# Output projection in two passes over the tokens, and a normalisation divided between it and the feed forward

## The reference

```python
y  = concat([out_a, out_b, out_c], -1) @ w_out[l]         # output projection; out_c is divided by its group RMS first
x  = layer_norm(ALPHA * x + g1 * y, ln1_g[l], ln1_b[l])   # g1, sh2, sc2, g2: adaLN vectors from c (c_ctx for the context)
h  = x * (1 + sc2) + sh2
x  = layer_norm(ALPHA * x + g2 * swiglu(h, w_gu[l], w_down[l]), ln2_g[l], ln2_b[l])
# the context tokens (ctx) go through the same in layer 0, and are dropped in layer 1
```

## Time and profile before

| | |
|---|---|
| median of 3 runs | 3813.87 us (3808.86 to 3818.49) |
| the profiled execution | 3815.01 us, span 3813.2 us, granted clock 0.944 |
| busy share | PE 88%, DVE 49%, POOL 36%, ACT 22% |
| stage out, layer 0, then layer 1 | from 927 to 1069 us, from 2889 to 3003 us |
| ffn up to the start of its second iteration | from 1070 to 1206 us, from 3004 to 3115 us |

### The profile page before, as it was taken

How to read it: one execution, slowest core, us unless ns; L and a number is a source line. 1 busy time by engine, 2 the same in 40 slices (tenths; PEclk the granted TensorE clock), 3 DMA queues, 4 the chain that set the end, 5 groups by cost and what they waited for, 6 DMA issues and landing times. The chain is left out here.

```text
span 3813.2 us, 47769 instructions
## 1 busy us (share of the span) xinstructions
PE 3362.3 (88%) x17208; PEld 2793.3 (73%) x17208; DVE 1866.7 (49%) x2854; ACT 846.7 (22%) x1574; POOL 1386.0 (36%) x1032
## 2 busy tenths in 40 slices
PE   0969989877979999999997669989787799999997
PEld 0849878655858888888884549878666578888885
DVE  8976534678582222222227886525675532222225
ACT  1136432212041010000003226432211220010102
POOL 1354222253324333343432254213242344444443
PEclk9979999988989999999998789999888899999998
DMA  7500002002301111111011410011002011111111
GB/s 278 171 17 1 0 30 65 6 20 89 118 28 39 39 39 39 33 41 42 33 33 67 171 61 1 0 39 56 6 14 86 33 40 49 50 50 50 44 50 50
DMA packets 63857, 197.74 MB, mean 52 GB/s; under 512 B 6160, under 2 KB 16656, under 8 KB 62736
## 3 DMA queue, kind: packets, MB, share of 16 engines
q1 hardware_dynamic: 54736, 172.32, 13.3%
q10 hardware_dynamic: 9024, 24.14, 1.8%
HBM read 177.05 MB, written 19.40 MB: 52 GB/s over the span
## 5 line engine op out<-in xcount | busy, mean ns | idle before, releaser
L188 PE MATMUL ps<-h_hi,f_whi 128*128 128x512 f32 (+1 forms) x1760 | 650.8, 370 | 26.5 <-DVE h_lo L1917 19.7
L189 PE MATMUL ps<-h_lo,f_whi 128*128 128x512 f32 (+1 forms) x1760 | 650.0, 369 | 0.0
L190 PE MATMUL ps<-h_hi,f_wlo 128*128 128x512 f32 (+1 forms) x1760 | 649.4, 369 | 0.0
L2145 DVE TENSOR_TENSOR f_gated<-f_gated,ps 128x512 f32<-128x512 f32 (+1 forms) x110 | 69.6, 634 | 973.8 <-PE ps L190 968.5
L2029 POOL TENSOR_TENSOR f_whi<-f_wraw,small 128x1024 fp32r<-128x1024 f32 x128 | 251.8, 1967 | 608.1 <-PE ps L190 608.1
L2153 DVE SCALAR_TENSOR_TENSOR x_res<-ps,mod,x_res 128x512 f32<-128x512 f32 (+1 forms) x440 | 306.8, 697 | 242.2 <-PE ps L190 241.9
L188 PEld LDWEIGHTS ps<-h_hi,f_whi 128*128 128x128 f32 x1760 | 333.3, 189 | 85.8 <-issue 22.2
L190 PEld LDWEIGHTS ps<-h_hi,f_wlo 128*128 128x128 f32 x1760 | 333.0, 189 | 55.8
L189 PEld LDWEIGHTS ps<-h_lo,f_whi 128*128 128x128 f32 x1760 | 333.3, 189 | 55.2
L188 PE MATMUL ps<-f_ahi,f_whi 128*128 128x512 f32 (+1 forms) x880 | 328.3, 373 | 0.0
L189 PE MATMUL ps<-f_alo,f_whi 128*128 128x512 f32 (+1 forms) x880 | 323.5, 368 | 0.0
(11 more groups left out here) (219 smaller groups left out, 6212.8 us busy)
## 6 DMA issues: line engine op xcount, KB each, us to landing
f_wraw<-in_w_ffn SPq DMA_DIRECT2D x132, 512.0 KB, 3.2
ada_w<-in_w_ada SPq DMA_DIRECT2D x80, 512.0 KB, 3.5
wrawc<-in_w_in SPq DMA_DIRECT2D x26, 512.0 KB, 3.8
wrawab<-in_w_in SPq DMA_DIRECT2D x16, 512.0 KB, 4.4
wrawo<-in_w_out SPq DMA_DIRECT2D x16, 512.0 KB, 3.4
ada_w<-in_w_ada ACTq DMA_DIRECT2D x16, 512.0 KB, 4.4
x_res<-in_xT SPq DMA_DIRECT2D x8, 640.0 KB, 6.5
x_spill<-x_res ACTq DMA_DIRECT2D x8, 640.0 KB, 5.6
```

The costliest lines, as they stand in the source:

```text
L188: pe.matmul(out, w_hi, h_hi, start=first, stop=False)
L189: pe.matmul(out, w_hi, h_lo, start=False, stop=False)
L190: return pe.matmul(out, w_lo, h_hi, start=False, stop=last)
L2145: dve.tensor_tensor(g, g, pl.bank(3 + c, tn), ALU.mult).then_inc(u_taken[c], 1)
```

## The change

`project_out` goes over the tokens twice. First it gathers and multiplies the early tokens (chunks 2 and 0; in layer 1 only chunk 0), output tiles 0 to 7; between those blocks PE turns the late tokens, chunk 1. Then it multiplies chunk 1, tiles 7 down to 0, in four banks that take turns. The last two weight tiles of the first pass serve the second as well; the other six are loaded and split again, so 14 tiles in place of 8. While the second pass runs, the early tokens are normalised: their mean and variance matmuls stand between its blocks, and centre, modulate and rest (in layer 1 the rescale too) stand among DVE's evictions. The first two weight tiles of the feed forward are loaded there too. The normalisation is now a class, `Norm`, with a step for each tile.

`feed_forward` normalises chunk 1 only, while PE runs gate and up of the early tokens for both inner tiles. Chunk 1 follows (for the second inner tile first, with a wait for each feature tile), which needs one weight tile once more. The rescale of the early tokens in layer 0 stands there as well. The 16 modulation tiles of layer 1 move out of layer 0's stage out into its ffn: `LaterModulation` does four products in each of iterations 1 to 8, with one buffer, its loads in ACT's queue and its products in DVE's.

```diff
--- before.py
+++ after.py
@@ -1628,137 +1628,411 @@
...
+        for k in range(KT):
+            dve.tensor_tensor(self.tile(c, k), self.tile(c, k), self.pl.bank(c, CHUNKS[c][1]),
+                              ALU.subtract).then_inc(self.centred[c], 1)
...
+    def modulate(self, dve, c, k):
...
+        dve.scalar_tensor_tensor(out=self.tile(c, k, self.pl.lo_f32), in0=self.tile(c, k),
+                                 scalar=self.gm[:, k, self.who(c)], in1=self.inverse(c),
+                                 op0=ALU.mult, op1=ALU.mult).then_inc(self.h_in[c], 1)
+
+    def rest(self, dve, c, k):
...
+        dve.scalar_tensor_tensor(out=self.tile(c, k, self.pl.lo), in0=self.tile(c, k, self.pl.lo_f32),
+                                 scalar=self.bm[:, k, self.who(c)], in1=raw(self.tile(c, k, self.pl.hi)),
+                                 op0=ALU.add, op1=ALU.subtract).then_inc(self.split[c], 1)
...
+    def block_bank(m, c):
+        return pl.bank(3 * (m % 2) + c if m < KT else (1, 4, 6, 7)[m % 4], CHUNKS[c][1])
+
+    def tile_of(m):
+
+        return m if m < KT else 2 * KT - 1 - m
+
+    def slot_of(m):
+        return m % 2 if m < KT else (m + 1) % 2
+
+    loads = [tile_of(m) for m in range(2 * KT) if m not in (KT, KT + 1)]
...
+                    sp.wait_ge(w_ready, m - 1)
+                sp.dma_start(w_raw[m % 2][:, :], a["w_out"][l, loads[m]]).then_inc(w_loaded[m % 2], 16)
+            load(0)
+            load(1)
+            sp.dma_start(pl.x[:, :, 0:width], pl.x_dram[:, :, 0:width]).then_inc(x_in, 16)
+            for m in range(2, KT + 2):
+                load(m)
+
+            sp.wait_ge(rest[1], len(items[1]))
+            for s in range(2):
+                sp.dma_start(ffn.early[s][:, :], a["w_ffn"][l, 0, s]).then_inc(next_in[s], 16)
+            for m in range(KT + 2, len(loads)):
+                load(m)
...
+            def split(p):
+                slot = p % 2 if p < KT else (p + 1) % 2
+                hi, lo = flat(w_hi[slot]), flat(w_lo[slot])
+                pool.wait_ge(w_loaded[p % 2], 16 * (p // 2 + 1))
+                if 2 <= p < KT:
+                    pool.wait_ge(full[0], p - 1)
+                elif p >= KT:
+                    pool.wait_ge(full[1], p - KT + 1)
+                pool.tensor_tensor(hi, w_raw[p % 2][:, :], one, ALU.mult).then_inc(w_rounded, 1)
+                pool.wait_ge(w_rounded, p + 1)
+                pool.tensor_tensor(lo, w_raw[p % 2][:, :], raw(hi), ALU.subtract).then_inc(w_ready, 1)
+            for p in range(KT + 1):
+                split(p)
+            for c in early:
+                norm.square_pairs(pool, c)
+            for p in range(KT + 1, len(loads)):
...
+            def multiply(m):
+                pe.wait_ge(w_ready, m + 1 if m < KT else max(KT, m - 1))
+                slot = slot_of(m)
+                for c in early if m < KT else late:
+                    t0, tn = CHUNKS[c]
+                    if 2 <= m < KT:
+                        pe.wait_ge(taken[c], m - 1)
+                    elif m >= KT + 4:
+                        pe.wait_ge(taken[c], m - KT - 3)
+                    for k in range(KT):
+                        mm = three_pass(pe, block_bank(m, c), w_hi[slot][:, k, :], w_lo[slot][:, k, :],
...
+            pe.wait_ge(rest[0], len(items[0]))
+            for m in range(KT):
+                multiply(m)
+                turn(1, m)
+            pe.wait_ge(rest[1], len(items[1]))
+            multiply(KT)
+            for c in early:
+                pe.wait_ge(norm.x_paired[c], KT // 2)
+                norm.mean(pe, c)
+            multiply(KT + 1)
+            norm.variance(pe, early[0])
+            multiply(KT + 2)
+            if not last:
+                norm.variance(pe, 0)
+            for m in range(KT + 3, 2 * KT):
...
+            for m in range(KT):
+                if m < 4:
+                    divide(1, m, m + 1)
+                evict(m)
+                rest_of(1, m)
+                if m % 2:
+                    for c in early:
+                        dve.wait_ge(taken[c], m + 1)
+                        norm.pair(dve, c, m // 2)
+            dve.wait_ge(next_rounded, 1)
...
+            evict(KT)
+            for c in early:
+                norm.centre(dve, c)
+            norm.invert(dve, early[0])
+            whole(norm.modulate, early[0])
+            whole(norm.rest, early[0])
+            evict(KT + 1)
+            evict(KT + 2)
+            if last:
+                norm.rescale(dve, 0)
+                evict(KT + 3)
+            else:
+                norm.invert(dve, 0)
+                whole(norm.modulate, 0)
+                evict(KT + 3)
+                whole(norm.rest, 0)
+            pair_late(3)
+            evict(KT + 4)
+            pair_late(2)
+            evict(KT + 5)
+            pair_late(1)
+            evict(KT + 6)
+            evict(KT + 7)
+            pair_late(0)
 
 
...
+    slot = [1, 0, 2, 1, 0, 2]
+    opening = [(0, early, 0), (1, early, 1), (2, early, 2), (3, early, 0),
+               (2, late, 2), (3, late, 0), (0, late, 2), (1, late, 1)]
+    blocks = [0, 1, 2, 3, 0, 4, 5]
+    homes = [0, 1, 2, 0, 2, 0, 2]
     n_down = KT * len(chunks)
     act_hi = pl.at(f"{tag}_ahi", [P, 2, TOK], F32R, kb=120)
     act_lo = pl.at(f"{tag}_alo", [P, 2, TOK], F32R, kb=130)
...
+            def split_opening(s):
+                pool.wait_ge(loaded[s % 2], 16 * (s // 2))
+                if s == 3:
+                    pool.wait_ge(gu_full[0], 1)
+                elif s >= 4:
+                    pool.wait_ge(gu_full[1], s - 2)
+                split(s - 1, s % 2, homes[s])
```

The opening of the feed forward on POOL, PE and DVE:

```diff
+            split_opening(2)
+            norm.square_pairs(pool, 1)
+            split_opening(3)
+            act_rest(0, 0, early)
+            act_rest(0, 1, early)
+            split_opening(4)
+            split_opening(5)
+            split_opening(6)
+            act_rest(0, 1, late, turn=0)
...
+
+            norm.mean(pe, 1)
+            for s, (j, part, place) in enumerate(opening):
+                if s == 1:
+                    norm.variance(pe, 1)
+                    pe.wait_ge(second_ready, 1)
+                elif s in (2, 3):
+                    pe.wait_ge(ready, s + 1)
+                elif s == 6:
+                    pe.wait_ge(ready, 5)
+                gate_up(0, j, part, place, None if s < 4 else (s - 4) // 2, norm.split[1] if s == 4 else None)
+            pe.wait_ge(ready, 7)
+            down(0, (homes[5], homes[6]))
...
+            norm.centre(dve, 1)
+            norm.invert(dve, 1)
+            for k in range(KT + 2):
+                if k < KT:
+                    norm.modulate(dve, 1, k)
+                if k == (2 if last else 4):
+                    gate(0, 0, early)
+                if k >= 2:
+                    norm.rest(dve, 1, k - 2)
+            gate(0, 1, early)
+            if carried is not None:
+                for c in early:
+                    carried.rescale(dve, c)
+                gate(0, 1, late, turn=0)
+                norm.rescale(dve, 1)
+            else:
+                norm.rescale(dve, 1)
+                gate(0, 1, late, turn=0)
+            gate(0, 0, late, turn=1)
+            if carried is not None:
+                for c in early:
+                    dve.wait_ge(carried.x_done[c], KT)
+            dve.wait_ge(norm.x_done[1], KT)
+            for c in chunks:
+                add(0, c)
+            for first, end, cond in loops:
+                with dve.Fori(first, end) as i:
+                    if cond is not None:
+                        ada.product(dve, cond, i, 0)
+                        ada.product(dve, cond, i, 1)
+                    gate(i, 0, chunks)
+                    if cond is not None:
+                        ada.product(dve, cond, i, 2)
+                        ada.product(dve, cond, i, 3)
```

And the products of layer 1's modulation, in DVE's queue ahead of the first gate product and between the first and the second (ACT's `ada.load` stands likewise, each load waiting for the product before it):

```diff
+                    if cond is not None:
+                        ada.product(dve, cond, i, 0)
+                        ada.product(dve, cond, i, 1)
+                    gate(i, 0, chunks)
+                    if cond is not None:
+                        ada.product(dve, cond, i, 2)
+                        ada.product(dve, cond, i, 3)
+                    gate(i, 1, chunks)
```

More of the change, by code:

```diff
@@ new lines, in _ @@
+            for p in range(2):
+                for n, (k, c) in enumerate(items[p]):
+                    t0, tn = CHUNKS[c]
+                    act.wait_ge(turned[p], n + 1)
+                    act.activation(pl.hi[:, k, t0:t0 + tn], pl.bank(gather_bank(p, n), tn), ACT.Copy,
+                                   scale=1.0 if k < 4 else gnorm(k)).then_inc(rounded[p], 1)
+            act.wait_ge(next_in[0], 16)
+            act.activation(ffn.hi[0][:, :], ffn.early[0][:, :], ACT.Copy).then_inc(next_rounded, 1)
@@ new lines, in _, with whole @@
+            dve.wait_ge(next_rounded, 1)
+            dve.tensor_tensor(ffn.lo[0][:, :], ffn.early[0][:, :], raw(ffn.hi[0][:, :]), ALU.subtract) \
+                .then_inc(next_split, 1)
```

(7 more changed lines are left out.)

550 lines of the change are left out of this document (361 added, 189 removed).

## The result

The changed kernel takes 3771.95 us (median of 4 runs, 3763.31 to 3779.39) for 3814.26 before: ratio 0.9886, 95% interval 0.9868 to 0.9905. I had said 3773. A second set of four gave 3771.65, ratio 0.9892 (0.9875 to 0.9908). The profiled run of the first set is its slowest, 3779.39; of the second, 3772.15.

A forecast was written before the change was run, and what follows sets the result against it. PE, 88% busy, was taken as the bound, waiting mainly in the gather and ffn's opening normalisation. Layer 0's 21.1 us and layer 1's 20.0 won, together 41.1 from 3815.0, gave 3773.9, so 3773 against the median; range 3747 to 3797.

The forecast's parts named there:

- Gather of layer 0: Ahead of layer 0's products: 12 divisions first, then rests, so products start 6.6 us earlier; layer 1's 11.0 earlier.
- 2.1 with none in the way: Layer 1's gather: division time in us if no POOL instruction intervenes; about 6 expected, 9.8 with all four.
- First passes: Early tokens' output products, with the wait for chunk 1's last rests: 75.4 us in layer 0, 51.2 in layer 1.
- Second pass of layer 1: Late blocks beside early normalisation: 43.6 of blocks, 6.8 of mean and variance, 11.3 of waiting, clock and last pair: 61.7 us.
- POOL's step is shut out until modulate and rest are over: Layer 1's second pass: tile 3's split waits behind DVE's 10.7 us stream, so PE waits 9.1 us, plus 1.7 of clock.
- My first rival: POOL gets its turn between DVE's instructions, so 22.3 us of waits and clock losses go: 3751 us; chance 25%.
- Second pass of layer 0: Late blocks 43.6, means and variances 10.2, waits of 0.6 and 2.8 us: 57.2 us.
- Gaps: Barrier from last product to first mean, with a last eviction, a pair and the stage change: 3.1 and 3.0 us.
- First parts: Feed forward to ffn's second iteration, with chunk 1's normalisation mostly covered: 101.0 us in layer 0, 77.1 in layer 1.
- The second idle in layer 0: Layer 0's ffn between late blocks: a split waiting behind DVE's rescale idles PE 5.3 us, plus 1.7 of clock.
- The products of the modulation: Layer 1's modulation products moved into layer 0's ffn iterations 1 to 8: cost nothing, or 58 us without cover.
- Rivals 2 and 3: Splits hold the second pass throughout, 3800 us, chance 10%; modulation's chain reaches PE in ffn's loop, 3831 us, chance 5%.

The follow-up runs named there:

- small splits: Changed kernel with the last five weight tiles of both second passes split in only 8 of 1024 columns: 3758.20 us, ratio to before 0.9845.
- evictions-first run: Changed kernel with layer 1's evictions of late blocks 9 and 10 ahead of rest, and block 11's ahead of rescale: 3770.28 us, ratio to before 0.9893.
- the run with eight: Changed kernel with GpSimd's split of the third late weight tile waiting until DVE has finished all eight modulate instructions: 3776.2 us, a single run.

## Why the prediction was right, and where it wasn't

The time was right, 3771.95 for 3773, and that it came within 1 us was luck, twice over. First, the touched stretches gave 48 us where I had 41, and what I took as unchanged was 4 to 13 us longer in the profiles (the rest 4.0 and 9.3, the stages ahead 0.8 and 4.1). The same code of the rest takes 1686.4 to 1694.1 in the twelve profiles since and 1683.0 in the only one of before. In all twelve, layer 1's attention has the largest part: 235.8 to 242.4 us at clocks of 0.96 to 0.99, for 232.9 at 1.00. Layer 0's attention, which runs ahead of anything changed, moves likewise, 255.4 to 260.7 at 1.00 to 0.98 (before 257.9), so one profile of before can't tell whether the change has a part in it; that is open. Second, a stall of about the predicted length came by a way that I hadn't seen, as told below.

Step by step, predicted and measured (first profile, then second):

- Gather of layer 0, 6.6 less: 7.2 and 7.2. Of layer 1, 11.0 less, 7 to 15: 14.8 and 13.2. Mechanism right for these two. That it hangs on when a load lands I had for layer 1 only, as "2.1 with none in the way", and without the lock-out: in layer 0 the same code takes 13.1 where the step comes 0.04 us later.
- First passes 75.4 and 51.2 with the wait at their end: 73.5 and 50.1 in the first profile, with PE busy 71.9 and 47.9 and 1.57 of waiting for the late rests, for 1.8. The 3 to 4 us of DVE a tile were covered, as said. In layer 1 PE waited 0.6 for a split besides.
- Second pass of layer 1, 61.7: 64.4 and 63.0. Here the step "POOL's step is shut out until modulate and rest are over" failed. I took 6.39 and 4.57 as what happens to any step that meets a stream. Those two had 25 and 27 gapless instructions behind them, mine 2. My first rival had this, "POOL gets its turn between DVE's instructions". But I let it cost nothing, and that was the other half of the error: four POOL steps in modulate and two in rest double DVE's streams, and I had not asked what stands behind them in DVE's queue. The evictions did: 10.4 of waiting where I had 9.1, by another way, and the same loss of clock behind it. The small splits and the evictions-first run show that way; the run with eight shows mine. Two smaller slips of the working: I had modulate begin 20.8 us into the pass and block 10 end 21.9 in, where they came 22.2 and 23.7 in, mostly since I counted 1.0 us of a variance that PE runs whole (3.6) behind block 9; and the stall, by my own 4.4 for a split, is 8.6 and not 9.1.
- Second pass of layer 0, 57.2 with 0.6 and 2.8 of waiting: 56.4 with one wait of 2.0, for a bank. Same failed step.
- Gaps 3.1 and 3.0: 6.1 and 2.8. In layer 0 DVE was still at the evictions and pairs behind the stretched modulate; with small splits it is 2.9.
- First parts 101.0 and 77.1: 99.1 and 74.1, later 98.3 and 75.5. (Layer 1's down projection is 22.2 "by the same ratio", not 21.8.) The second idle in layer 0 came, 3.5 for 5.3. It was for the gate product behind a rescale of 18.79 us for 16 instructions, not for a split:

```profile
1130.94 18.79 DVE L1709 SCALAR_TENSOR_TENSOR x_res<-x_res,n_ga,n_ri 128x256 f32<-128x256 f32 x16
1149.65 0.68 DVE L2530 TENSOR_TENSOR f_gated<-f_gated,ps 128x512 f32<-128x512 f32 x1
```

- The products of the modulation, nothing: ten iterations to the loops' end take 835.6 us for 834.95 before, with 256.5 us of DVE in them for 197.0. Rivals 2 and 3 are out; PE waited for no product, and for no split in any late block of the changed kernel.

Of rival 1's sum of 22.3 us to be had if no stall came, 13 to 17 were there: the small splits show them.

The Trainium skill ("SBUF — State Buffer", who interferes with whom) says that whoever issues first holds the shared pair for one whole instruction. For POOL's steps with up to 6 DVE instructions behind, this kernel agrees: one instruction each, 0.74 us stretched to 2.4 or 2.9. With 7 and more POOL's step waits for several instructions, which that sentence doesn't give, and the measurement decides: 6.88 us for a step of 1.9.

## What to carry to other kernels

Where two engines slow each other, ask for both what stands behind the slowed one in its own queue: the price is paid by whoever waits for that, here banks freed by evictions. Put what another engine waits for (an eviction, a gate product) ahead of a long stream, and cut the stream into the slots in which the waiting engine is paced by something else. And before a slow row is carried to another place, compare what had gone before it there: here the number of instructions in the run.

## What the runs showed of the hardware

- A GpSimd step that reads SBUF and meets a gapless DVE run with two SBUF inputs gets its turn when DVE has at most 6 instructions of the run behind it (over a hundred steps in thirteen profiles, at most one whole instruction more to wait), and waits for the run's end when it has 7 or more and at least two to go (23 steps, 7 to 29 behind, 3.2 to 6.9 us for steps of 0.2 to 2.4). A DVE instruction that was itself held up starts the count anew; evictions from PSUM within the run don't, though they let a waiting step in (with eight, it ran beside the two behind rest). Beside these, each profile of a changed kernel has one 256-token step that came with 16 behind and only one instruction to go, which fits both. Why there is such a count wasn't tried.
- Division (one SBUF input, in place, 0.26 us each) behaves alike: steps that came 1.78 us or less into the run took their turn, steps from 1.82 us on waited for its end. In both cases 6 instructions were finished and the seventh was under way. Between two profiles of the same code in the gather, a step that came 0.04 us later into the divisions went with a gather 7.6 us shorter.
- Each turn costs DVE nearly the whole GpSimd step: 12.95 us for 8 instructions of 5.38 with four steps between, which alone take 1.9 and 2.4 us in turn, 8.6 together. Steps of 0.2 us cost nothing that can be seen (5.39).
